# Zeroed expert rows, early gathers, halved first reloads and adding scatters in an encoder layer

## The reference

```python
g_idx = argmax(xt @ w_rg + b_rg)                     # one of 4 groups
top_v, top_i = top_k(e_logits of that group, 2)      # two of its 8 experts
top_w = softmax(top_v) * p(group)
h = silu(xt @ w_gate[e]) * (xt @ w_up[e])            # 1024 -> 256
out = sum over the two experts of top_w * (h @ w_down[e])   # 256 -> 1024
x = x + out;  return rms_norm(x, norm_final)
```

## Time and profile before

| | us |
|---|---|
| median of 3 runs | 641.47 (641.33 to 643.52) |
| the profiled execution | 638.51 |
| its span in the trace | 636.6 |
| TensorE busy | 582.1 (91%) |
| VectorE busy | 270.8 (43%) |
| ScalarE busy | 209.0 (33%) |
| GpSimd busy | 84.2 (13%) |
| DMA, mean over the span | 239 GB/s |

### The profile page before, as it was taken

How to read it: one execution, slowest core, us unless ns; L and a number is a source line. 1 busy time by engine, 2 the same in 40 slices (tenths; PEclk the granted TensorE clock), 3 DMA queues, 4 the chain that set the end, 5 groups by cost and what they waited for, 6 DMA issues and landing times.

```text
span 636.6 us, 8580 instructions
## 1 busy us (share of the span) xinstructions
PE 582.1 (91%) x3399; PEld 442.2 (69%) x3400; DVE 270.8 (43%) x589; ACT 209.0 (33%) x404; POOL 84.2 (13%) x119
## 2 busy tenths in 40 slices
PE   3999999999999999999999966899999998788894
PEld 3789878888588888888888854566666665444552
DVE  3646558645434557433362476211211211103365
ACT  3545547554496733422251241011111111000112
POOL 3000404000002101100000122212212211111002
PEclk9999999999989999999999995899999999989998
DMA  7475120402213213168788296899999999999993
GB/s 246 94 262 186 43 66 1 132 2 67 66 34 100 66 39 95 34 192 291 294 320 333 91 353 280 315 380 420 421 425 422 425 424 424 423 426 424 425 386 133
DMA packets 57017, 152.17 MB, mean 239 GB/s; under 512 B 8184, under 2 KB 38160, under 8 KB 44304
## 3 DMA queue, kind: packets, MB, share of 16 engines
q1 hardware_dynamic: 51840, 141.53, 57.9%
q0 software_dynamic: 5008, 9.99, 4.2%
q10 hardware_dynamic: 128, 0.09, 0.1%
HBM read 147.37 MB, written 12.60 MB: 251 GB/s over the span
## 4 chain that ended last, share of the span: by engine, by line
PE 74%; DVE 7%; DMA 7%; SPq 6%; ACT 2%; issue 2%; POOL 1%; POOLq 0%; ACTq 0%; DVEq 0%
PE bank L717 40%; PE bank L1096 11%; SPq L482 6%; PE bank L710 5%; PE bank L1116 5%; DMA slots<-expert_w_up 5%; PE bank L1170 2%; PE bank L812 1%; DVE softmax L1667 1%; DMA xg<-hn_rows,gcolm 1%; PE bank L892 1%; DMA x_in<-x 1%; PE bank L1188 1%; PE bank L790 1%; ACT squares L1555 1%
## 5 line engine op out<-in xcount | busy, mean ns | idle before, releaser
L1096 PE MATMUL bank<-slots,xgT 128*64 128x256 f32 x544 | 78.9, 391 | 2.6 <-DMA slot2b<-expert_w_up 1.9
L1678 DVE TENSOR_TENSOR w_low<-w,w_high 128x1024 fp32r<-128x1024 f32 x32 | 39.2, 1225 | 80.0 <-ACT w_high L1337 80.0
L717 PE MATMUL bank<-x_high,w_high 128*128 128x512 f32 x168 | 67.6, 402 | 1.0 <-DVE x_low L1605 1.0
L1096 PEld LDWEIGHTS bank<-slots,xgT 128*64 128x64 f32 x544 | 51.9, 141 | 22.2 <-issue 5.1
L717 PE MATMUL bank<-x_high,w_low 128*128 128x512 f32 x168 | 66.4, 395 | 0.0
L717 PE MATMUL bank<-x_low,w_high 128*128 128x512 f32 x168 | 66.1, 394 | 0.0
L1966 DVE COPY y<-bank 128x512 f32<-128x512 f32 x14 | 9.7, 692 | 97.7 <-PE bank L1116 97.7
L1337 ACT ACTIVATE w_high<-w 128x1024 fp32r<-128x1024 f32 x32 | 33.7, 1054 | 53.2 <-PE bank L717 53.2
L717 PE MATMUL bank<-w_high,x_high 128*128 128x420 f32 x128 | 45.3, 354 | 0.0
L717 PE MATMUL bank<-w_high,x_low 128*128 128x420 f32 x128 | 45.3, 354 | 0.0
L717 PE MATMUL bank<-w_low,x_high 128*128 128x420 f32 x128 | 45.2, 353 | 0.0
(11 more groups left out here) (277 smaller groups left out, 1177.6 us busy)
## 6 DMA issues: line engine op xcount, KB each, us to landing
slots<-expert_w_gate SPq DMA_DIRECT2D x20, 1024.0 KB, 17.3
slots<-expert_w_up SPq DMA_DIRECT2D x18, 1024.0 KB, 6.3
slots<-expert_w_down SPq DMA_DIRECT2D x16, 1024.0 KB, 19.1
slot2b<-expert_w_down SPq DMA_DIRECT2D x9, 1024.0 KB
w<-w_in SPq DMA_DIRECT2D x16, 512.0 KB, 3.7
slot2b<-expert_w_up SPq DMA_DIRECT2D x8, 1024.0 KB, 24.7
slot2b<-expert_w_gate SPq DMA_DIRECT2D x8, 1024.0 KB, 26.8
w<-w_in SPq DMA_DIRECT2D x8, 840.0 KB, 4.6
```

What stands on the lines that cost most here:

```text
L717: ins_ = mm(out_, stat[a_], mov[b_], start=first and q_ == 0, stop=last and q_ == 2)
L1096: ins = mm(bank[2][e * SLOTS:(e + 1) * SLOTS, m * FE:(m + 1) * FE], xgT[:, c, e * SLOTS:(e + 1) * SLOTS], gu[m][e][:, c], start=(c == 0), ...
L1678: V.tensor_tensor(wl2[:, u % 2, :], raw2[:, u % 2, :], wh2[:, u % 2, :].bitcast(F32), ALU.subtract).then_inc(s["lo_done"], 1)
```

## The change

- A buffer of zeros, `nil_rows`, stands behind the ring's fourth place of `slot2b`, where part 6 will be loaded. GpSimd zeroes it at the start, and SyncE writes it eight times to `expert_rows` (512 KB each), behind the units 2 to 9. Part 6 is loaded after these stores have landed, behind unit 17. All of `expert_rows` is zero from there on.
- The two scatters of zeros are gone, and `first_gather(1)` follows `first_gather(0)`. Counts of `hn_out`, `xg_zero` and `zcol_done` are adapted.
- The first four reloads (parts 21 to 24, into the places of pair 0's gate and up) are issued in halves of 512 KB: the first halves when TensorE has done half of the products of gate or up, the second ones after all. `arrived` counts the landings.
- The scatters of pairs 0 to 13 add to the rows in HBM instead of overwriting them.

```diff
+        nil_rows = place_at(RING2 + 4 * PART, "nil_rows", D)[:, :]
...
+        HALVED = range(R, R + 4)
+        ZERO_PIECES = 2 * NT
+        arrived = {(n_, m_): sum(32 if q_ in HALVED else 16 for q_, (p_, w_, _) in enumerate(order)
+                                 if w_ == m_ and p_ % 4 == n_ % 4 and p_ <= n_) for n_ in range(PAIRS) for m_ in range(3)}
...
+            def load_half(q, h):
+                pair, m, e = order[q]
+                cols = slice(h * PART // 2, (h + 1) * PART // 2)
+                sp.dma_start(ring[q % R][:, cols], (g_rows, u_rows, d_rows)[m][:, 2 * pair + e, cols]).then_inc(m_in[pair % 4][m], 16)
+
             sp.wait_ge(s["lo_done"], 2 * len(jobs))
-            load_part(6)
+            sp.wait_ge(s["xg_zero"], 1)
             FREE = 18
             for u in range(FREE):
                 load_unit(u)
+                if 2 <= u < 2 + ZERO_PIECES:
+                    sp.dma_start(z_dram[(u - 2) * P:(u - 1) * P, :], nil_rows).then_inc(s["hn_out"], 16)
+            sp.wait_ge(s["hn_out"], 16 * ZERO_PIECES)
+            load_part(6)
...
-                sp.wait_ge(s[("g_done", "u2_done", "dn_done")[m]], (n + 1) * (2 if m == 2 else 1))
-
-            for q in range(R, 6 * PAIRS):
+                sp.wait_ge(s[("g_done", "u2_done", "dn_done")[m]], 2 * (n + 1) if m == 2 else n + 2)
+
+            for m in range(2):
+                for h in range(2):
+                    sp.wait_ge(s[("g_done", "u2_done")[m]], h + 1)
+                    for e in range(2):
+                        load_half(R + 2 * m + e, h)
+            for q in range(R + 4, 6 * PAIRS):
...
+            nc.gpsimd.memset(nil_rows, 0.0).then_inc(s["xg_zero"], 1)
...
-                                        bounds_check=2 * SEQ - 1, oob_is_err=False).then_inc(s[f"scattered{k}"], 16)
+                                        bounds_check=2 * SEQ - 1, oob_is_err=False, compute_op=ALU.add).then_inc(s[f"scattered{k}"], 16)
...
             first_gather(0)
+            first_gather(1)
             pool.wait_ge(s["tabs_done"], 1)
 
-            for i in range(PAIRS - LAST):
-                nc.gpsimd.tensor_copy(zcol[:, i:i + 1], ztab[:, LAST + i:LAST + i + 1]).then_inc(s["zcol_done"], 1)
-                pool.wait_ge(s["zcol_done"], i + 1)
-                pool.indirect_dma_start(out=z_dram, out_offset=bass.IndirectOffsetOnAxis(ap=zcol[:, i:i + 1], axis=0),
-                                        in_=xg[1], in_offset=None,
-                                        bounds_check=2 * SEQ - 1, oob_is_err=False).then_inc(s["v_out"], 16)
-            pool.wait_ge(s["v_out"], 48)
-            first_gather(1)
             gather(2, 2, 0, True)
...
-                ins.then_inc(s[("g_done", "u2_done")[m]], 1)
+                    if c == KC - 1 or (halved and c == KC // 2 - 1):
+                        ins.then_inc(s[("g_done", "u2_done")[m]], 1)
```

More of the change, by code:

```diff
@@ L531, in _ @@
             load_part(11)
-            sp.wait_ge(s["hn_out"], 16 * NT)
+            sp.wait_ge(s["hn_out"], 16 * (ZERO_PIECES + NT))
             sp.wait_ge(s["hT_done"], 2 * NT)
@@ L624, in _ @@
                 inverse_root(rstd2[:, t:t + 1], ss2[:, t:t + 1], D).then_inc(s["rstd_done"], 1)
-            pool.wait_ge(s["hn_out"], 16 * NT)
+            pool.wait_ge(s["hn_out"], 16 * (ZERO_PIECES + NT))
             pool.wait_ge(s["hT_done"], 2 * NT)
@@ L629, in _ @@
                 nc.gpsimd.memset(xg[k], 0.0).then_inc(s["xg_zero"], 1)
-            pool.wait_ge(s["xg_zero"], 2)
+            pool.wait_ge(s["xg_zero"], 3)
             def gather(t, n, k, prev):
@@ L648, in scatter @@
                 pool.sem_inc(s["pool_step"], 1)
-                pool.wait_ge(s["zcol_done"], n + 3)
+                pool.wait_ge(s["zcol_done"], n + 1)
                 pool.sem_inc(s["pool_step"], 1)
@@ L1085, in turn_x, with gate_or_up @@
                         ins.then_inc(s["xt_done"], 1)
-            def gate_or_up(n, m, own, k, loads):
+            def gate_or_up(n, m, own, k, loads, halved=False):
                 gu, _ = slot_views(own)
-                pe.wait_ge(m_in[k][m], 32 * loads)
+                pe.wait_ge(m_in[k][m], loads(m))
                 for c in range(KC):
@@ L1109, in down @@
                 pe.wait_ge(s["hTs_done"], n + 1)
-                pe.wait_ge(m_in[k][2], 32 * loads)
+                pe.wait_ge(m_in[k][2], loads(2))
                 pe.wait_ge(s["y_outA"], n + 1)
@@ L1120, in weights_of @@
             def weights_of(n):
-                return n, n % 4, n // 4 + 1
+                return n, n % 4, lambda m: arrived[n, m]
             turn_x(0, 0, 1)
-            gate_or_up(0, 0, *weights_of(0))
+            gate_or_up(0, 0, *weights_of(0), halved=True)
             for n in range(LAST):
-                gate_or_up(n, 1, *weights_of(n))
+                gate_or_up(n, 1, *weights_of(n), halved=(n == 0))
                 if n + 1 < LAST:
@@ L1147, in _ @@
                             turn_x(n, 2, dv + 1)
-                            gate_or_up(n, 0, None, 1, dv + 5)
-                            gate_or_up(n, 1, None, 1, dv + 5)
+                            gate_or_up(n, 0, None, 1, lambda m: 32 * (dv + 5))
+                            gate_or_up(n, 1, None, 1, lambda m: 32 * (dv + 5))
                             turn_h(n)
-                            down(n, None, 1, dv + 5)
+                            down(n, None, 1, lambda m: 32 * (dv + 5))
                             pe.reg_add(done, done, 1)
@@ L1492, in silu @@
             def silu(n):
-                act.wait_ge(s["u2_done"], n + 1)
+                act.wait_ge(s["u2_done"], n + 2)
                 A(h_silu, bank[2][:, 0:FE], ACT.Silu).then_inc(s["silu2_done"], 1)
```

## The result

| | median, us | against the kernel before |
|---|---|---|
| before | 641.4 (4 runs) | |
| changed | 648.09 (644.96 to 652.07, 4 runs) | 1.0151 (1.0109 to 1.0192) |

The account below looks back on a forecast made before the run. The prediction took DMA time in the experts' stage as the bound. Additions cost 8.3 us, gathers and halves gain 3.9, stores 0: 4.4 us later than 641.47, so 645.9 us, range 637.0 to 654.0.

Parts of the forecast that it names:

- What bounds the kernel: Projections and attention until 360 us are TensorE's; the experts' full stretch from 424 us is bound by DMA time.
- A row's byte costs what a weight byte costs: In the experts' full stretch, gathered and scattered rows displace weight loads byte for byte, at 424 GB/s.
- I take one read more per row at the price of a gathered byte ... 8.3 us: The adding scatters in the experts' stage read 3.54 MB more at 424 GB/s: 8.3 us later.
- The rivals of hidden and half hidden reads: Expert scatters' destination reads run beside the loads: wholly, 637.6 us, chance 0.18; partly, 641.6 us, chance 0.27.
- read and write in turn: Rival for the expert scatters: each added row costs two copies more, +16.6 us, giving 654.2 us; chance 0.10.
- Gains together: 3.9 us: At the start of the experts, 1.0 + 1.2 + 1.7 us saved by gathers and halved reloads; bounds 1.3 and 5.1.
- I take 1.2 us as regained: Loads ran short at 412 to 416 us and before 424 us; TensorE 4.5 us earlier from pair 1 regains 1.2 us.
- the stream starts at 398.8, 1.7 us earlier: Halved first reloads start the expert weight stream after half of pair 0's gate, gaining 1.7 us; bounds 0 and 2.2.
- the gathers' 1.0 us: Gathers of pairs 1 and 2 move into the DMA hole before the full stretch, saving 1.0 us; bounds 0.6 and 1.3.
- Stores, part 6, zeroing: Zero stores in the attention stage, the late part 6 load and GpSimd's extra zeroing cost 0; bounds 0 and +1 us.
- Latency has room: Expert scatters landing in 10 to 13 us instead of 8.0 delay nothing; even 16 us would cost nothing.
- The sum: Over the whole kernel, additions less gains, 8.3 - 3.9 = 4.4 us later, put on the median: 645.9 us.

Follow-up runs that it names:

- its twin: The changed kernel with scatters that overwrite instead of add (stores, early gathers and halves kept): 638.41 us, ratio 0.9998 to the kernel before.
- the doubled ones: The changed kernel with every adding scatter and every zero store issued twice, the second into another tensor: 665.53 us, ratio 1.0429 to the kernel before.
- the kernel with whole reloads: The changed kernel with overwriting scatters and the first reloads whole instead of in halves (stores, early gathers kept): 637.6 us, ratio 0.9992 to the kernel before.
- two sets: The changed kernel with overwriting scatters and the eight zero stores issued twice, the second into another tensor: 637.52 us, ratio 0.9987 to the kernel before.

## Why the prediction was right in its sign and half in its size

*What bounds the kernel:* right. All that moved the time clear of noise moved the rate or the bytes of the full stretch, and what lay in TensorE's stage (the stores) moved nothing that can be told.

*A row's byte costs what a weight byte costs:* right, measured alone: 8.6 us for 3.67 MB, by the rule 8.7.

*"I take one read more per row at the price of a gathered byte ... 8.3 us":* borne out in its size, as far as it can be told. By the times it is 9.8 us twice (the changed kernel against its twin, 6.7 to 12.9; half of the doubled ones) and 11.2 once (8.4 to 14.0). By the software queue's time it is 8.9 us, and 9.3 with the doubled ones. By the rates it is 8.1 us. 8.3 counts 13.5 of 14 scatters, all of them are 8.7, and that lies inside each of the three intervals. So an added row costs about two copies; whether it is a little more isn't shown, nor is it shown that the read, and not the adding, takes the time. The rivals of hidden and half hidden reads are out by the doubled additions, and read and write in turn (16.6 us) is above all three intervals.

The Trainium skill ("Collectives: The Full Stack", section "The bandwidth ceiling: the fold count and why AG ≠ RS ≠ AR") has two source reads set the price of an addition. The runs agree with the factor: a whole addition cost 17.8 us, and twice the 8.6 us of a copy is 17.2. The Trainium skill ("DMA: Bandwidth & Descriptors", section "Where 436 GB/s comes from") puts a ceiling at the SBUF ports, by which, as the prediction read it, the read from HBM would have been free; the 403 and 387 GB/s decide against that here. The same section of the Trainium skill lets a lower limit of HBM, about 358 GB/s, bind between HBM and SBUF, which the prediction left out; the 423 GB/s of this stream, with one core working, lie above it.

*"Gains together: 3.9 us":* this is the term that was mis-sized. Measured 0.6 us against the stores alone, with 2.3 either way, and 0.1 us against the kernel before, with 1.7 either way; 2.2 us by the traces. Three parts:

- *"I take 1.2 us as regained"* for the two gaps in the loads, and the 4.5 us on TensorE behind it: both stood on one execution, in which pair 1's gather landed late and the clock then fell. Two further traces of the same kernel have neither; the trace of the stores alone has both, that of stores and additions has no late gather. What the change removes there is a mishap that came in two of five traces, no steady cost.
- *"the stream starts at 398.8, 1.7 us earlier"*: the start is nearly right (2.9 us after the gate forecast, 3.0 and 3.2 measured, 2.9 to 3.6 in all traces with early halves). The worth is not: the first halved loads run below a full share (0.79) for 4 us and then at 366 instead of 422 GB/s, so that 16 us after the gate nothing is left of the lead. The prediction had written that the queue doesn't empty, which was so from 8 us after the gate on (share 0.98 to 1.04), and had read that as full rate. By the times the halves bring nothing (0.9998 with them, 0.9992 with whole reloads, 2.5 us either way).
- *the gathers' 1.0 us*: left within what can be told. The kernel with whole reloads is 1.0 us ahead of the stores alone (with 2.5 either way), by its one trace 2.4 ahead of the mean without early gathers.

*Stores, part 6, zeroing:* 0 forecast, +0.5 us measured with 1.6 either way, and no more with two sets.

*Latency has room:* right. Scatters land in 9.4 us instead of 8.0 (10 to 13 forecast), the row reads were issued from 605.5 us on, and the tail took 45.7 us as before. The scatters of the changed kernel, which answer to the earlier trace rows:

```profile
L671 POOL DMA_INDIRECT expert_rows<-y,zcol x14: 1577/1606/1633, 420.0 to 594.5; - x14
...
DMA to landing us min/median/max: 8.7/9.4/10.4
```

*The sum:* 8.3 - 3.9 = 4.4 was forecast. 9.8 - 0.1 = 9.7 was measured, the 0.1 being what stores, gathers and halves bring together against the kernel before (ratio 0.9998). The gains' size has the larger part of the miss, 3.8 us of 5.3; the other 1.5 are the addition, and they are within the noise of the 9.8.

*The absolute time:* 645.9 us was forecast and 648.09 measured, and that it is so near is in part luck. The forecast stood on a median of three runs, 641.47 us, about 3 us above the level of the 69 later runs, and this hid a good half of the 5.3 us by which the change came out dearer. The last `up` weights were forecast to land near 595.3 us; they landed at 602.05, 3.4 of the 6.8 us from the low clock ahead of the experts. And the prediction's range doesn't quite take in the upper end of the addition's cost, as it says: that end is 654.2 us by its own sum, the range ends at 654.0.

## What to carry to other kernels

In a stage where the DMA engines are full, a scatter that adds cost about as much here as two that overwrite, although the MB in the profile stayed the same: look at the GB/s of the stretch at a share of 1, and at the queue's time. Where each row is written once and the target needn't keep what it held, as here, a plain overwrite does the same for half the price. A gap seen in one trace is worth its length only if a second trace of the same kernel has it too; look for what was issued just before it. And a queue that is busy isn't a queue at full rate: count the bytes, not the start.

## What the runs showed of the hardware that was not expected

- What a scatter costs by adding appears in no byte count, only in the queue's time: 9.45 MB in 34.3 us of 16 engines with additions, 4.0% of 634.7 us, 25.4 us, with overwrites, in 4720 packets each. GpSimd's own instruction took 1.6 us instead of 1.0.
- The first 512 KB loads after a stretch with few transfers moved 280 to 400 GB/s at a DMA share near 1; the same pieces in a running stream 410 to 422.
- A row gather landed after 7.2 and 8.1 us in the two traces in which the first 1 MB load was issued before GpSimd's gather instruction had ended, and after 3.8 to 3.9 us in the three in which it came at its end or later.
- The granted clock between 170 and 200 us differed from one execution to the next. The same products took 35.4 to 40.4 us over all traces, 35.4 to 37.1 in three of the kernel before, whose 69 later runs spread over about 8 us.
